# Third mixer: the rotary halves of queries and keys exchanged by transfers in memory

## The reference

```
p = h @ ab_w_in
qa, ka, va = split_cols(p[..., :A_COLS], A_SIZES)
oa = diff_attention(qa, ka, va, diff_lam, diff_subln, lambda_init(layer), cos, sin)
ob = rwkv7_time_mix(p[..., A_COLS:], ...)
mix = concatenate([oa, ob], axis=-1) @ ab_w_out
```

## Time and profile before

| | us |
|---|---|
| median of 3 runs | 2870.78 |
| lowest and highest | 2868.59, 2872.48 |
| profiled execution | 2868.78 |
| its span | 2867.0 |
| TensorE busy | 2704.0 |
| VectorE busy | 1509.2 |
| ScalarE busy | 986.6 |
| GpSimd busy | 350.5 |

### The profile page before, as it was taken

The page is one execution under the profiler, slowest core; times in us unless marked ns, Lnnn a source line. Parts: engine busy times, 40 slices in busy tenths (PEclk is TensorE's granted clock), DMA queues, the critical chain, the costliest instruction groups (busy, mean ns, idle before and its releaser), DMA issues.

```text
span 2867.0 us, 32354 instructions
## 1 busy us (share of the span) xinstructions
PE 2704.0 (94%) x13312; PEld 2142.0 (75%) x13312; DVE 1509.2 (53%) x2062; ACT 986.6 (34%) x1662; POOL 350.5 (12%) x306
## 2 busy tenths in 40 slices
PE   7879998999999988899999999999999977999998
PEld 6767876788888665586788888888878534788886
DVE  7965897544334678546434334343365367543333
ACT  3214654422222533543322223222233335332221
POOL 0001001222200001000222102221000000122200
PEclk9979999999999998799999999999999878999999
DMA  3333112122232221001333332223322200133232
GB/s 137 76 83 127 62 53 70 65 98 99 97 96 93 74 67 47 8 2 61 102 99 100 96 98 94 96 96 100 98 92 96 68 15 1 52 104 100 98 94 83
DMA packets 77539, 229.04 MB, mean 80 GB/s; under 512 B 16976, under 2 KB 18256, under 8 KB 77136
## 3 DMA queue, kind: packets, MB, share of 16 engines
q1 hardware_dynamic: 64464, 213.51, 22.9%
q0 software_dynamic: 1840, 5.77, 1.1%
q10 hardware_dynamic: 11088, 7.70, 0.9%
HBM read 221.18 MB, written 5.77 MB: 79 GB/s over the span
## 4 chain that ended last, share of the span: by engine, by line
PE 79%; DVE 13%; ACT 5%; issue 1%; DMA 1%; ACTq 1%; POOL 0%; DVEq 0%; POOLq 0%
PE ps L354 78%; DVE mem L371 5%; DVE part L441 2%; ACT part L429 1%; PE ps L365 1%; DVE mem L384 1%; DMA mem<-lag_dram 1%; DVE mem L2887 1%; DVE mem L377 1%; DVE ps L371 1%; ACTq L1139 1%; DVE mem L389 1%; DVE mem L549 0%; ACT mem L505 0%; DVE mem L630 0%
## 5 line engine op out<-in xcount | busy, mean ns | idle before, releaser
L354 PE MATMUL ps<-part,part 128*128 128x512 f32 (+2 forms) x9918 | 2277.4, 391 | 41.3 <-DVE part L441 18.2
L354 PEld LDWEIGHTS ps<-part,part 128*128 128x128 f32 x9918 | 1855.1, 189 | 461.1 <-DVE part L441 22.0
L441 DVE TENSOR_TENSOR part<-mem,part 128x1024 fp32r<-128x1024 f32 (+2 forms) x421 | 561.2, 1340 | 579.6 <-ACT part L429 579.1
L429 ACT ACTIVATE part<-mem 128x1024 fp32r<-128x1024 f32 (+2 forms) x421 | 417.5, 1002 | 224.6 <-DMA mem<-in_ffb_down 56.7
L371 DVE TENSOR_TENSOR mem<-ps,mem 128x512 f32<-128x512 f32 (+2 forms) x296 | 195.6, 661 | 345.3 <-PE ps L354 335.7
L354 PE MATMUL ps<-mem 128*64 128x64 f32 (+13 forms) x2568 | 273.1, 317 | 60.3 <-DVE mem L371 29.3
L354 PEld LDWEIGHTS ps<-mem 128*64 128x64 f32 (+4 forms) x2568 | 185.3, 169 | 138.8 <-issue 54.5
L513 POOL TENSOR_TENSOR mem<-mem 128x512 f32<-128x512 f32 x62 | 80.8, 1304 | 1132.5 <-ACT mem L505 1131.5
L1557 ACT ACTIVATE part<-mem 128x512 fp32r<-128x512 f32 x88 | 55.6, 632 | 328.5 <-DVE mem L371 328.5
L371 DVE TENSOR_TENSOR mem<-mem 128x512 f32<-128x512 f32 (+10 forms) x289 | 141.8, 491 | 43.2 <-ACT mem L1584 11.4
L1554 ACT ACTIVATE mem<-mem 128x512 f32<-128x512 f32 x88 | 55.6, 632 | 314.2 <-DVE mem L371 314.2
(11 more groups left out here) (178 smaller groups left out, 1060.8 us busy)
## 6 DMA issues: line engine op xcount, KB each, us to landing
mem<-in_ffa_gate SPq DMA_DIRECT2D x44, 512.0 KB, 3.2
mem<-in_ffa_up SPq DMA_DIRECT2D x44, 512.0 KB, 3.2
mem<-in_ffb_gate SPq DMA_DIRECT2D x44, 512.0 KB, 3.2
mem<-in_ffb_up SPq DMA_DIRECT2D x44, 512.0 KB, 3.2
mem<-in_ffa_down SPq DMA_DIRECT2D x32, 512.0 KB, 3.5
mem<-in_ffb_down SPq DMA_DIRECT2D x32, 512.0 KB, 3.6
mem<-in_w_odd SPq DMA_DIRECT2D x24, 512.0 KB, 3.2
mem<-in_w_ab SPq DMA_DIRECT2D x22, 512.0 KB, 3.2
```

The source lines that it names most:

```text
L354: return e.matmul(out, l, r, start=start, stop=stop, skip_group_check=True)
L429: w.e.activation(K.wts[c % NH].h[:, 0:n], K.raws[c % NR][:, 0:n], ACT.Copy).then_inc(*K_A.up(("w", c)))
L441: w.e.tensor_tensor(t.l, K.raws[c % NR][:, 0:n], t.hf, SUB).then_inc(*K.V.up(("w", c)))
```

## The change

Only the third mixer is changed, with the tables that it shares with the last one.

- The eight rotations on TensorE are gone. GpSimd instead issues, for each query and key product, four transfers of 32 partitions by 512 columns (64 KB) from ScalarE's copy to a second buffer, the halves exchanged (`turn_gpsimd`). The buffer is `K.nb[2]` for even ones and `wa` for odd ones.
- `turned_vector` waits for these and multiplies them by the sines in place. The signs are now in the table of sines and no longer in `rot`.
- On GpSimd's queue seven of the eight stand ahead of `d1`. The last, key 3, stands between `d1` and the wait for it.
- `g2` is loaded behind the attention's last step on ScalarE, since `wa` is in use before.
- VectorE waits for its own last operation when the tables of cosines and sines for the keys have been made.

```diff
@@ -169,7 +169,7 @@
 
         self.sems = [sem(n) for n in ("tensor_sums", "vector_out", "scalar_out", "gpsimd_out")]
         inputs = ("consts", "consts1", "params0", "params", "x0", "x1", "x2", "x3", "x4", "x5", "x6", "x7", "ssm_bc", "pool_w", "w2a2", "g2", "nsa_w2")
-        moved = ["raw0", "raw1", "shuffle", "out", "lag_zeros", "lags_out", "lags_in"]
+        moved = ["raw0", "raw1", "shuffle", "turned0", "turned1", "out", "lag_zeros", "lags_out", "lags_in"]
         moved += [f"{n}{tl}" for n in ("u_out", "u_in", "y_out", "y_in") for tl in range(4)]
         self.dma_sems = {n: sem(f"{n}_landed") for n in inputs + tuple(moved)}
         self.prm = ctx.enter_context(nc.sbuf_tensor("prm", [P, NCOL], F32))
@@ -1593,6 +1593,24 @@
     tt(w, dst, dst, prod, ADD, (name, "rope", o))
 
 
+def turn_gpsimd(K, w, name, o, raw, turned, which):
+
+    w.wait_ge(*K.A[name, o])
+    for r in range(4):
+        a = 32 * (r ^ 1)
+        w.e.dma_start(turned[32 * r:32 * r + 32, :], raw[a:a + 32, 0:T]).then_inc(
+            *K.counts[f"turned{which}"].up((name, o), by=16))
+
+
+def turned_vector(K, w, name, o, dst, raw, turned, which, cos, sin):
+
+    w.wait_ge(*K.A[name, o])
+    w.e.tensor_tensor(dst, raw[:, 0:T], cos, MUL).then_inc(*K.V.up())
+    w.wait_ge(*K.counts[f"turned{which}"][name, o])
+    w.e.tensor_tensor(turned, turned, sin, MUL).then_inc(*K.V.up())
+    tt(w, dst, dst, turned, ADD, (name, "rope", o))
+
+
 class Ab:
 
 
@@ -1624,8 +1642,8 @@
         self.lam = m.flat(8)
         self.mu1, self.ka1, self.sub = m.flat(14), m.flat(4), m.flat(1)
         self.rope = [self.raw[0], self.raw[1]]
-        self.cos, self.sin, self.prod = K.nb[0], K.nb[1], K.nb[2]
-        self.lt = self.prod[:, 0:64]
+        self.cos, self.sin, self.turned = K.nb[0], K.nb[1], [K.nb[2], self.wa]
+        self.lt = K.nb[2][:, 0:64]
         self.factors = K.nb[2]
         sets = [self.vt[:, i, :] for i in range(4)] + [spare[:, 0:T], spare[:, T:2 * T]]
         self.sets = [sets[0:3], sets[3:6]]
@@ -1816,17 +1834,12 @@
     for first, name in ((0, "q"), (4, "k")):
         for o, _ in enumerate(linear(K, w, name, 4, 8, K.h, h_ready, K.A)):
             n = first + o
-            if o:
-                rope_tensor(K, w, name, o - 1, E.rope[(o - 1) % 2], T)
-            elif n:
-                rope_tensor(K, w, "q", 3, E.rope[1], T)
             if n < 2:
                 ab_lower_tensor(K, w, n)
             if n == 1 or n == 2:
                 ab_bonus_tensor(K, w, n + 1)
             if n == 4 or n == 6:
                 ab_lower_tensor(K, w, n // 2)
-    rope_tensor(K, w, "k", 3, E.rope[1], T)
     linear_tok(K, w, "av", T, K.h, h_ready, K.A)
     ab_attention_tensor(K, w)
 
@@ -2124,6 +2137,7 @@
         if o == 4:
             tt(w, E.cos, K.cc("cos"), K.rstd, MUL)
             tt(w, E.sin, K.cc("sin"), K.rstd, MUL)
+            w.wait_ge(*K.V.now)
     weights_lo(K, w, c + 25)
     ab_rope_vector(K, w, 7)
     weights_lo(K, w, c + 26)
@@ -2199,7 +2213,7 @@
     E = K.ab
     name, o = ("q", n) if n < 4 else ("k", n - 4)
     dst = E.q if n < 4 else E.k
-    rope_vector(K, w, name, o, dst[:, o, :], (E.rope[o % 2], E.prod), T, E.cos, E.sin)
+    turned_vector(K, w, name, o, dst[:, o, :], E.rope[o % 2], E.turned[o % 2], o % 2, E.cos, E.sin)
 
 
 def rwkv_b_vector(K, w, i):
@@ -2343,9 +2357,6 @@
         if o == 0:
             ab_rates_scalar(K, w, 3)
         ab_rope_scalar(K, w, o)
-        if o == 0:
-            w.wait_ge(*K.P["rate", 3])
-            e.dma_start(E.g2, K.io["g2"]).then_inc(*K.counts["g2"].up("landed", by=16))
         if o == 1 or o == 2:
             ab_decays_scalar(K, w, o + 1)
         if o == 4 or o == 5:
@@ -2355,6 +2366,8 @@
         w.wait_ge(*K.P["av", t])
         e.activation(E.vt[:, t, :], K.acc("av", t), ACT.Copy, scale=K.rT[:, t:t + 1]).then_inc(*K.A.up(("av", t)))
     ab_attention_scalar(K, w)
+    w.wait_ge(*K.V["k", "rope", 3])
+    e.dma_start(E.g2, K.io["g2"]).then_inc(*K.counts["g2"].up("landed", by=16))
     weights_hi(K, w, c + 28)
 
     for i in range(18):
@@ -2423,8 +2436,13 @@
     memset(w, E.pads, 0.0, "pads_ab")
     d1, d2 = K.scratch
     S = K.counts["shuffle"]
+    w.wait_ge(*K.P["kk", 3])
+    w.wait_ge(*K.P["rate", 3])
+    for n in range(7):
+        turn_gpsimd(K, w, "q" if n < 4 else "k", n % 4, E.rope[n % 2], E.turned[n % 2], n % 2)
     w.wait_ge(*K.V["L", 3])
     e.dma_start(d1.rearrange("c s u t -> (c s) u t"), E.L).then_inc(*S.up("d1", by=16))
+    turn_gpsimd(K, w, "k", 3, E.rope[1], E.turned[1], 1)
     w.wait_ge(*S["d1"])
     for q in range(4):
         e.dma_start(E.M[32 * q:32 * q + 32, :, :], d1[q].rearrange("s u t -> u s t")).then_inc(*S.up("M", by=16))
@@ -3225,14 +3243,14 @@
     R = np.zeros((P, P), f)
     for b in (0, 64):
         for d in range(32):
-            R[b + d + 32, b + d] = -1
+            R[b + d + 32, b + d] = 1
             R[b + d, b + d + 32] = 1
     put("rot", R)
     inv = (10000.0 ** (-np.arange(0, 64, 2, dtype=f) / 64)).astype(f)
 
     def tabs(pos):
         ang = pos.astype(f)[None, :] * np.tile(inv, 4)[:, None]
-        return np.cos(ang), np.sin(ang)
+        return np.cos(ang), np.sin(ang) * np.where(i % 64 < 32, -1, 1)[:, None]
 
     a, b = tabs(np.arange(T))
     put("cos", a)
```

## The result

The changed kernel took 2861.17 us (median of 8 runs) against 2870.93 before; the ratio is 0.9962, with an interval of 0.9951 to 0.9972. Two more sets of runs of the same pair gave 0.9980 (0.9969 to 0.9991) and 0.9968 (0.9956 to 0.9979). So it is faster by about 0.3%, the mean of the three being 8.6 us. The forecast was 5.1 us less and "within 0.2%". The size was missed in the mean of the three; whether the range held differed from one comparison to the next. The profiled execution took 2858.0 us.

What follows compares the result with a forecast made beforehand. TensorE with its rotations, then VectorE, was taken to bound the third mixer. Gains of 1.9 (first hand-over) and 6.5 (rotations and bank), less 3.3 (late inverse), gave 5.1 us less: 2865.7 us, range 2861.5 to 2870.5.

Steps and rivals of the forecast that it cites:

- What bounds the stage: Third mixer: the chain of waits runs through TensorE's rotations and two VectorE pieces between them; after about 1108 VectorE carries it.
- The first hand-over: TensorE's gap before lower product 1: four transfers in 5.0 us replace waiting for a rotation, 1.9 us gained (0.1 to 2.5).
- The clock: Granted clock falling in the gap before lower product 1: some 2 us cost, left as it is.
- The seven rotations: TensorE from lower product 1 on: seven rotations at 0.85 us each removed, 6.0 us gained (5.2 to 6.7).
- the bank's wait of 0.48 us: TensorE's idle time before key product 0, gone because a long-empty bank is used; 6.5 us gained together with the rotations.
- The inverse held by key 3: GpSimd's queue: key 3's turning delays the loads of `M`, so the attention starts 3.3 us later (2.4 to 5).
- The output gate's weights: Their load moves behind the attention on ScalarE's queue: nothing taken, 0.3 us at most.
- Rival 4: GpSimd's issues each wait for a VectorE operation: four transfers land at 7.5 us, 1.9 us slower, 2872.7 us; chance 0.05.
- From there on every row stands 5.1 us earlier: After the attention's start, put at 1102.8, everything later was taken to shift by the same 5.1 us.
- Rival 2: Quick transfers or a clock that stays up: 6.4 us gained, up to 2 more from the clock, 2862.4 us; chance 0.40.

Runs made afterwards that it cites:

- Lower first: Changed kernel with VectorE emptying lower product 0 ahead of query 0's rotary step: 73.65 us from query 0's copy to the attention's first sum, ratio to before 0.9954.
- inverse first: Changed kernel with SyncE issuing the loads of `M`, and weights' low parts and the inverse's part 0 ahead of key 3's rotary step: ratio to before 0.9972.
- key 3 by a product: Changed kernel with key 3 alone turned by TensorE's product again: 76.99 us from query 0's copy to the attention's first sum, ratio to before 0.9965.
- M by SyncE: Changed kernel with SyncE, not GpSimd, issuing the four loads of `M` behind the wait for `d1`: ratio to before 0.9978.
- eight issues: Changed kernel with each turning as eight transfers of 16 partitions instead of four of 32: ratio to before 0.9990.
- no turning: Changed kernel without the transfers of turned rows, VectorE multiplying the unturned copy by the sines (rotary step not computed): ratio to before 0.9959.
- tables and gate: Kernel before, rotations kept, with only the signs moved into the sine tables and the output gate's weights loaded later: ratio to before 1.000.
- key 3 by a product, lower first: Changed kernel with key 3 turned by TensorE's product and lower product 0 emptied ahead of query 0's rotary step: ratio to before 0.9972.

## Why the prediction was wrong, step by step

- **What bounds the stage**: right. The rotations were on the chain, and the two hand-overs to VectorE were the places where it was decided.
- **The first hand-over**: mis-sized. I took 5.0 us for four transfers, the middle between 4.1 and 5.9. They took 4.0: the copy ended at 1021.42 and the last of them landed at 1025.4, 0.2 us before VectorE's sine product at 1025.66, with 0.50 us an issue and 1.9 to land. The single `u_dram` transfer, from which the lower end of 4.1 came, was the better neighbour; the four that ended after 5.9 us go in pieces of 512 bytes, and no run separates the pieces' part in that. The upper end of 2.5 us came, and 0.2 more, half of it since VectorE went from the cosine to the sine product without a pause. That is 0.8 us of the error. The fit from the Trainium skill, "DMA: Bandwidth & Descriptors", section "Anatomy of one DMA — SWDGE (gpsimd) path", set beside the sum there, gave 3.7 us and was nearer than my 5.0; the whole 2.5 us were gained, as the sentence on it said.
- **The clock**: mis-sized. I left its cost as it was. Lower product 1 took 1.87 us against 2.08 and query product 2 6.43 against 6.66: less of the work fell in the low stretch, which gave back 0.4 us of the some 2. With the rotations this made 5.5 us where 5.0 was reckoned. "Lower first" gave back the other 1.5.
- **The seven rotations, and the bank's wait of 0.48 us**: right. There is no idle row between the products after lower product 1. (The 6.5 us are 6.0 and 0.48, rounded up.)
- **The inverse held by key 3**: right, to a tenth. `M` was met 9.9 us after key product 3 ended (1070.9 to 1080.78), as worked out; VectorE came 3.7 us after the scores instead of 3.3. TensorE's scores came 0.4 us sooner behind key product 3 than reckoned, which is the difference. Taking the turning away gave 2.9 us back.
- **The output gate's weights, taken at nothing**: right. With them and the tables alone the ratio is 1.000.
- **Rival 4's price**: its landing after 7.5 us does not follow from its terms. Three issues of 1.22 us in place of 0.53 put 2.1 on the 5.0, so 7.1, and 1.4 us slower in all and not 1.9. Issues did not stretch (0.50 us each, the longest 0.55), so nothing hangs on it.
- **"From there on every row stands 5.1 us earlier"**: this is the step that failed, beside the 1.4 us in the stage. It took all that follows as fixed, a term put at nothing without a reason. From the first sum of the attention to the last load for this mixer's output took 240.4 us in the three profiles of before and 241.5 in the three of the changed kernel, so 1.1 was given back; from there to the last load of `w_cd` it is 866.8 and 867.5, another 0.7. The last mixer took 5.5, 8.0 and 4.1 us less in the three pairs of profiles. What is left of the 10.8 us between the first pair of spans, 1.9 ahead of the stage and -1.3 behind the last mixer, is within what these stretches move between executions of one kernel. In the last mixer no instruction differs; the granted clock does. Windows of TensorE behind the last load of `w_cd` (stretch, length, busy, granted clock, DMA share, GB/s), in the third profile of before and then of the changed kernel:

```profile
2249.20:2256.20 7.00, 7.00 (x54) 0.85 0.24 77
2256.20:2263.20 7.00, 7.00 (x10) 0.50 0.46 150
2263.20:2270.20 7.00, 5.52 (x11) 0.50 0.00 1
2270.20:2277.20 7.00, 6.00 (x23) 0.93 0.00 0
```
```profile
2244.60:2251.60 7.00, 7.00 (x55) 0.95 0.26 80
2251.60:2258.60 7.00, 7.00 (x11) 0.50 0.51 150
2258.60:2265.60 7.00, 5.52 (x14) 0.82 0.00 1
2265.60:2272.60 7.00, 5.43 (x34) 1.00 0.00 0
```

Both tables start at the same place in the work. In windows of 1 us the clock is low there for 17 us in each of the three profiles of before, and for 10 us in each of the three of the changed kernel; it falls 1.3 us later and comes back 5.5 us sooner, and the work behind it stands 2.8 us earlier. Later stretches are shifted as well. Over this mixer the mean is 0.85 to 0.87 against 0.90, or 68 to 75 us at the low level against 51.

**What stays open.** Why the low stretches lie otherwise, and what the changed kernel gains by them in every execution. With "inverse first" the last mixer was short too (248.8 us). In the other six kernels with a shorter stage it was not: 254.5 to 255.7 us in "key 3 by a product", the two with "lower first", "M by SyncE" and "eight issues", and 256.9 in "no turning". Their stages run from 73.65 to 83.46 us, on both sides of the changed kernel's, so the short mixer does not follow from the stage's length in any simple way. One thing goes together in all 14 profiles: where 866.8 us lie ahead of the last load of `w_cd` (the three of before, "tables and gate", "M by SyncE", "no turning", "lower first"), the first low stretch behind it lasts 17 us, and where 867.5 do, 10. So part of the clock's pattern is already settled before the last mixer; no run shows by what.

The whole times speak for some gain outside the stage, and weakly. The three ratios mean 8.6 us; 6.5 less 1.1 and 0.7 leaves 3.9 for the last mixer, at the lower end of the 4.1 to 8.0 of the profiles. The interval of each of the three reaches some 3 us to either side, and the second alone (5.7 us) would need nothing from the last mixer. In the table the ratios follow the stage only roughly: "key 3 by a product, lower first" has one of the shortest stages and a middling ratio.

The chances were the other fault. Rival 2, faster by over 0.2%, had 0.40 and came true. The quick transfers were as it said, and 0.4 us of its clock; its rotations at their upper end were not needed, and the part made in the last mixer is in no rival and was luck. The forecast stood 0.6 us from the line between the two, and the range's lower end had room for the stage's favourable ends but none for work outside it.

## What to carry to other kernels

A product that only exchanges rows of 32 partitions can go to transfers where its result is not needed for some 4 us, or 5 to 6 where they meet another queue's load (key 0 in the changed kernel, key 3 in "M by SyncE"). Then place its issues with care, because on an in-order queue they hold up what stands behind them (here 2.9 us in front of four loads that a long chain waits for: 2 of issues and 0.9 of waiting for the copy). Before taking work off an engine, look at what the other engine does between the event that it waits for and the one that it releases: one line moved in VectorE's order gave another 5 us, which the whole rewriting had left untouched. And where untouched stages show stretches of low granted clock, as here, leave a few microseconds in the range for them.

## What the runs showed of the hardware

- Transfers from one part of the on-chip memory to another, 32 partitions of 2 KB: 0.50 us an issue on GpSimd's queue, 1.9 us to land (1.8 to 3.7), with VectorE's products and sums running beside them. VectorE's products took 0.69 us beside them, as before. The warning in the Trainium skill, "SBUF — State Buffer", section "SBUF: two separate sides", that a VectorE operation in a two-port mode keeps GpSimd from writing descriptors, names fp32 copies as the trigger. The operations here were of two operands, and the longest of the 32 issues took 0.55 us; no run here had a copy within the memory beside such an issue, so the warning itself was not tested.
- A small transfer that meets another queue's load can take twice its time: 3.5 and 3.8 us against 1.8 to 1.9 beside a load of weights ("eight issues", query 0), and 3.5 to 4.1 against 1.9 to 2.0 beside SyncE's loads of `M` in pieces of 128 bytes ("M by SyncE", key 3). Eight of half the size that met no load were there 5.1 us after the first issue, and four of the full size 3.4.
- The granted clock's first low stretch in the last mixer was 17 us long in the three profiles of before and 10 us in the three of the changed kernel; later ones moved between executions of one kernel too. Stretches that were not touched came out 1.1 us longer (behind the changed kernel's attention), 2.8 to 3.3 us longer (behind that of "inverse first", "eight issues" and both kernels with the product for key 3: 243.2 to 243.8 us against 240.4), and up to 8 us shorter (the last mixer).
